# Two 4-block transpositions of a fused decoder kernel: from TensorE to block turns and moves

## The reference

```
y = rms(h) ; z = y @ w_in                      # 2048 -> 4096, in four mixers
oa = spatial unit(za)   : gelu(u) * (W_s @ layernorm(gelu(v)) + b_s)   # 512 wide
ob, oc, od              : short convolution, conformer, pooling        # 512 wide each
h = h + concat(oa, ob, oc, od) @ w_out         # the output projection
h = h + (silu(y @ w_gate) * (y @ w_up)) @ w_down
h = h + sigmoid(y @ w_ple_gate) * (p @ w_ple_proj) ; x1 = rms(h)
q, k, v, gate = rms(x1) @ swa_w_in             # the attention's input
h = x1 + (softmax(q k + bias, sinks) v * silu(gate)) @ swa_w_out
```

## Time and profile before

| | us |
|---|---|
| median of 3 runs | 1383.69 |
| lowest and highest | 1382.33, 1383.71 |
| the profiled execution, its own time | 1381.95 |
| its span | 1380.2 |
| TensorE busy in it | 1373.5 |
| VectorE busy | 1150.4 |
| ScalarE busy | 866.6 |

### The profile page before, as it was taken

The page is one execution under the profiler, slowest core; times in us unless marked ns, Lnnn a source line. Parts: engine busy times, 40 slices in busy tenths (PEclk is TensorE's granted clock), DMA queues, the critical chain, the costliest instruction groups (busy, mean ns, idle before and its releaser), DMA issues.

```text
span 1380.2 us, 16996 instructions
## 1 busy us (share of the span) xinstructions
PE 1373.5 (100%) x6191; PEld 1124.8 (81%) x6191; DVE 1150.4 (83%) x1394; ACT 866.6 (63%) x1162; POOL 152.2 (11%) x127
## 2 busy tenths in 40 slices
PE   9999999999999999999999999999999999999999
PEld 7888888888888888788888888888888887777887
DVE  6589976788999988899999889976777669886898
ACT  7476755566777555677756577655565556665554
POOL 2000010011111000111100011100000144430000
PEclk9999999999999999999999999999999999999999
DMA  9777656887999788899987889998878688889685
GB/s 332 249 209 216 199 174 228 284 234 252 297 277 267 226 260 256 249 279 264 280 267 248 245 255 251 276 321 295 253 236 279 219 263 259 262 257 289 204 251 173
DMA packets 181419, 349.80 MB, mean 253 GB/s; under 512 B 12913, under 2 KB 36717, under 8 KB 181208
## 3 DMA queue, kind: packets, MB, share of 16 engines
q1 hardware_dynamic: 158968, 289.56, 63.9%
q0 software_dynamic: 9280, 33.97, 12.6%
q10 hardware_dynamic: 13088, 25.18, 5.9%
HBM read 295.14 MB, written 26.26 MB: 233 GB/s over the span
## 4 chain that ended last, share of the span: by engine, by line
PE 96%; DVE 2%; DMA 1%; ACT 0%; issue 0%; POOL 0%; ACTq 0%; POOLq 0%; DVEq 0%
PE acc L2150 15%; PE acc L2152 14%; PE acc L2151 14%; PE acc L2334 13%; PE acc L2336 13%; PE acc L2337 13%; PE sp L2334 2%; PE sp L2336 2%; PE tp L2336 2%; PE tp L2334 2%; PE tp L2337 2%; PE sp L2337 2%; DMA wide<-w_raw 1%; DVE w_lo L1380 1%; PE acc L2212 1%; PE sp L2449 1%
## 5 line engine op out<-in xcount | busy, mean ns | idle before, releaser
L952 ACT ACTIVATE w_hi<-w_raw 128x1024 fp32r<-128x1024 f32 x453 | 474.2, 1057 | 310.2 <-PE acc L2152 209.7
L1380 DVE TENSOR_TENSOR w_lo<-w_raw,w_hi 128x1024 fp32r<-128x1024 f32 x431 | 522.3, 1226 | 155.0 <-ACT w_hi L952 152.4
L2150 PE MATMUL acc<-w_lo,hh 128*128 128x512 f32 x528 | 207.9, 394 | 0.0
L2152 PE MATMUL acc<-w_hi,hl 128*128 128x512 f32 x528 | 205.7, 390 | 0.0
L2151 PE MATMUL acc<-w_hi,hh 128*128 128x512 f32 x528 | 205.6, 389 | 0.0
L2334 PE MATMUL acc<-w_lo,yh 128*128 128x512 f32 x452 | 176.0, 389 | 0.0
L2336 PE MATMUL acc<-w_hi,yh 128*128 128x512 f32 x452 | 175.9, 389 | 0.0
L2337 PE MATMUL acc<-w_hi,yl 128*128 128x512 f32 x452 | 175.8, 389 | 0.0
L952 ACT ACTIVATE w_hi<-wide 128x1024 fp32r<-128x1024 f32 x104 | 110.3, 1060 | 72.0 <-DVE wide L1394 33.5
L1380 DVE TENSOR_TENSOR w_lo<-wide,w_hi 128x1024 fp32r<-128x1024 f32 x104 | 126.8, 1223 | 14.9 <-ACT w_hi L952 14.6
L2150 PE MATMUL acc<-w_lo,yh 128*128 128x512 f32 x352 | 137.4, 390 | 0.0
(11 more groups left out here) (336 smaller groups left out, 2180.3 us busy)
## 6 DMA issues: line engine op xcount, KB each, us to landing
w_raw<-in_w_gate SPq DMA_DIRECT2D x88, 512.0 KB, 5.7
w_raw<-in_w_up SPq DMA_DIRECT2D x88, 512.0 KB, 6.3
w_raw<-in_w_down SPq DMA_DIRECT2D x88, 512.0 KB, 6.4
w_raw<-in_w_in SPq DMA_DIRECT2D x64, 512.0 KB, 4.5
wide<-w_raw POOLq DMA_DIRECT2D x52, 512.0 KB, 5.7
w_raw<-in_swa_w_in ACTq DMA_DIRECT2D x48, 512.0 KB, 5.2
w_raw<-in_w_out SPq DMA_DIRECT2D x32, 512.0 KB, 5.5
w_raw<-in_w_ple_gate SPq DMA_DIRECT2D x32, 512.0 KB, 5.2
```

Source lines behind the costliest of these rows:

```text
L952: act.activation(w_hi[:, v % SPL], src, ACT.Copy).then_inc(hi_ready, 1)
L1380: dve.tensor_tensor(w_lo[:, v % SPL], src, w_hi[:, v % SPL].bitcast(F32), ALU.subtract).then_inc(lo_ready, 1)
L2150: pe.matmul(dst, xh[:, f, tk], w_lo[:, v % SPL, k], start=(f == 0), stop=False)
L2152: last = pe.matmul(dst, xl[:, f, tk], w_hi[:, v % SPL, k], start=False, stop=(f == CK * n - 1))
```

## The change

Both results are turned and moved instead of transposed on TensorE. The indices of the moved tiles go up by one (`T_OA = 0`, and a fourth `T_SWA`), the two pairs of PSUM halves go.

In the output projection `turn` follows the products on VectorE at (0, 0), the move stands on SP behind load 7, ScalarE's and VectorE's readings stay at (0, 3), and the first unit uses the spatial quarter last: short convolution, pooling, conformer, spatial.

In the attention `turn` follows `add_gated(3)` at (0, 3), the move stands on SP behind load 12, ScalarE makes the high half at (0, 6) and VectorE the low half at (0, 7), both behind the split of that step. The first two units are interleaved: chunks 0 to 5 of unit 0, 0 to 3 of unit 1, 6 and 7 of unit 0, 4 to 7 of unit 1. ScalarE takes unit 0 at (1, 7) instead of (1, 3).

```diff
+OUT_FIRST = (0, 1, 2, 3, 6, 7, 4, 5)
+SWA_STEPS = [(0, c) for c in range(6)] + [(1, c) for c in range(4)] + [(0, 6), (0, 7)] + [(1, c) for c in range(4, 8)]
+SWA_STEPS += [(v, c) for v in range(2, 9) for c in range(8)]
...
+LAST_CHUNK[SWA_UNIT] = OWN[START[SWA_UNIT] + SWA_STEPS.index((0, 7))] + 1
...
-T_FFN, T_HID, T_PLE, T_SWA, T_K, T_OG = 0, 4, 15, 19, 22, 23
+T_OA, T_FFN, T_HID, T_PLE, T_SWA, T_K, T_OG = 0, 1, 5, 16, 20, 24, 25
@@ SP
-                    load(START[OUT_UNIT + j] + c, wout_v, OUT_ROWS[c], CW * j)
+                    load(START[OUT_UNIT + j] + c, wout_v, OUT_ROWS[c if j else OUT_FIRST[c]], CW * j)
+                    if (j, c) == (0, 7):
+                        move(T_OA)
...
-                v, c = divmod(s, 8)
+                v, c = SWA_STEPS[s]
                 load(ATT + s, swi_v, CK * c, CW * SWA_ORDER[v])
                 if s == 4:
                     move(T_SWA + 2, freed=T_SWA)
+                if s == 12:
+                    move(T_SWA + 3, freed=T_SWA + 1)
@@ ScalarE
                     if (j, c) == (0, 3):
-                        high(H_OA, hh[:, 8:12])
+                        turned_high(T_OA, hh[:, 8:12])
...
-                    if (v, c) == (0, 5):
-                        high(H_SWA, hh[:, 12:16], gfs[:, 12:16])
+                    if (v, c) == (0, 6):
+                        swa_turned_high(3)
...
-                    if (v, c) == (1, 3):
+                    if (v, c) == (1, 7):
                         act.wait_ge(prod, 2)
                         take(SWA_UNIT, tok(0), ACT.Copy, rr)
@@ VectorE
                         last.then_inc(oa_ready, 1)
+                        dve.wait_ge(oa_ready, 1)
+                        turn(T_OA, tok(5))
...
-                        low(H_OA, hl[:, 8:12], hh[:, 8:12])
+                        turned_low(T_OA, hl[:, 8:12], hh[:, 8:12])
...
                     if (v, c) == (0, 3):
                         add_gated(3)
+                        dve.wait_ge(x1_ready, 4)
+                        turn(T_SWA + 3, resid[:, :, 3 * CW:])
                     if (v, c) == (0, 5):
-                        low(H_SWA, hl[:, 12:16], hh[:, 12:16], gfs[:, 12:16])
                         request(R_FIN, 32)
...
+                    if (v, c) == (0, 7):
+                        swa_turned_low(3)
@@ TensorE
-                for c in range(8):
-                    u = OUT_UNIT + j
+                for i in range(8):
+                    u, c = OUT_UNIT + j, i if j else OUT_FIRST[i]
...
                     if j == 0 and c == 4:
-                        wait_half_left(pe, H_OA + 1)
+                        pe.wait_ge(turned_lo, T_OA + 1)
...
-                    chunk(START[u] + c, u, c, hh, hl)
-                    if (j, c) == (0, 1):
-                        pe.wait_ge(oa_ready, 1)
-                        to_features(H_OA, tok(5))
+                    chunk(START[u] + i, u, c, hh, hl, end=None if j else OUT_FIRST[-1])
...
-                    if v == 0 and c in (0, 2, 4):
-                        pe.wait_ge(turned_lo, T_SWA + c // 2 + 1)
-                    if (v, c) == (0, 6):
-                        wait_half_left(pe, H_SWA + 1)
+                    if v < 2:
+                        j, k = SWA_STEPS[8 * v + c]
+                        if j == 0 and k % 2 == 0:
+                            pe.wait_ge(turned_lo, T_SWA + k // 2 + 1)
+                        chunk(START[u] + c, SWA_UNIT + j, k, hh, hl)
+                        continue
                     chunk(START[u] + c, u, c, hh, hl)
-                    if (v, c) == (0, 2):
-                        pe.wait_ge(x1_ready, 4)
-                        to_features(H_SWA, resid[:, :, 3 * CW:])
```

More of the change, by code:

```diff
@@ L222 @@
         LAST_CHUNK[_block.unit + _role] = _block.last(_role) + 1
-HALVES = "d" + "fx" + "xx" * 3 + "d" + "dx" + "aa" + "xx" + "dd" + "aa" + "xx"
-H_MIX, H_X, H_VEC, H_INIT, H_PZ, H_PO, H_CB, H_CN, H_OA = 0, 1, 9, 10, 12, 14, 16, 18, 20
+HALVES = "d" + "fx" + "xx" * 3 + "d" + "dx" + "aa" + "xx" + "dd" + "aa"
+H_MIX, H_X, H_VEC, H_INIT, H_PZ, H_PO, H_CB, H_CN = 0, 1, 9, 10, 12, 14, 16, 18
 M_HC, M_SC, M_BG = range(3)
-H_SWA = len(HALVES)
-HALVES += "xx"
 H_Q, H_PV = {}, {}
@@ L2138, in _, with chunk @@
         def _(pe):
-            def chunk(s, u, c, xh, xl, by_bank=None):
+            def chunk(s, u, c, xh, xl, by_bank=None, end=None):
                 if c == 0 and u >= 2:
@@ L2144, in chunk @@
                 wait_low(pe, v)
-                n = UNITS[u][0]
+                end = UNITS[u][0] - 1 if end is None else end
                 for t in range(T):
@@ L2152, in chunk @@
                         last = pe.matmul(dst, xl[:, f, tk], w_hi[:, v % SPL, k], start=False,
-                                         stop=(f == CK * n - 1))
+                                         stop=(f == CK * end + CK - 1))
                     if by_bank is not None:
```

## The result

The change makes the kernel slower: a median of 1386.43 us over 8 runs (1385.77 to 1389.00) against 1383.53 over 8 runs of the kernel before (1382.33 to 1385.11). The ratio is 1.0028, with a 95% interval of 1.0019 to 1.0037: 3.9 us, between 2.6 and 5.1. The medians lie 2.9 apart, against the +3.1 that was forecast. The profiled execution took 1386.48 around a span of 1384.4; the kernel before, 1381.95 around 1380.2.

The account below looks back on a forecast made before the run. TensorE, busy in all of the span, was taken to bound the kernel. No gain from the first removal, +0.5 and +2.6 us from the moves (0.92 returned included) gave +3.1: 1386.8 us, range 1384.3 to 1389.7.

Parts of the forecast that it names:

- The removal at the first place: Output projection: dropping the transposes gains 0, as step 2 waits for the same low half; bounds 0 and 0.9 us.
- The first move: Output projection: the spatial tile returns at 213.4, delaying step 4's weights queued behind it; +0.5 us, bounds 0 and +3.4.
- The second move: Attention: the late tile holds up weights of steps 7 and 8; +2.6 us net, bounds +2.0 and +3.2, +5.5 with slow reads.
- Not slower: Rival, attention step 8: the tile returns before ScalarE asks, a move of 6.0 us instead of 9.1; 1383.3, chance 0.2.
- The clock falls: Rival: the 2.8 us wait puts TensorE at 1.2 GHz for a chunk, 2.7 us more; 1389.5, chance 0.1.
- The sum: Both places: +0.5 and +2.6 make +3.1 us, 1386.8 in terms of the median; forecast's own span +2.0 to +4.4.
- What was priced at nothing: Interleaved units, unit 0 taken four chunks later, the attention tile's low half before step 10: each covered, 0.
- the 0.92: Attention: TensorE time of the eight removed transposes, 0.92 us, said to come back and already counted in the +2.6.

Follow-up runs that it names:

- second_alone: The changed kernel with only the attention's edits, the spatial unit's output transposed on TensorE again: median 1387.26 us, 1.0031 of the kernel before.
- move_behind_11: The changed kernel with SP's move of the attention's last quarter behind load 11 instead of load 12: median 1382.16 us, 0.9999 of the kernel before.
- late_tables: `late_and_early_split` with the second and third of GpSimd's bias tables sent later: median 1381.53 us, 0.9993 of the kernel before.
- late_halves: The changed kernel with ScalarE's and VectorE's halves of the attention's fourth tile made later, at (1, 1): median 1383.02 us, 1.0005 of the kernel before.
- late_and_early_split: `late_halves` with ScalarE's conformer work in the output projection one step later, behind step 2's high half: median 1382.90 us, 1.0000 of the kernel before.
- first_alone: The changed kernel with only the output projection's edits, the attention's last quarter transposed on TensorE again: median 1382.78 us, 0.9998 of the kernel before.

## Why the prediction was right, and where not

**The removal at the first place, 0:** right. Step 2 waits for the same low half, 0.74 in the change and 0.77 alone, and starts at 210.93 instead of 210.89.

**The first move, +0.5:** wrong, it cost 0. The step that failed is "The nearest write, at 1052.17, landed in 4.4". This one landed in 2.64, with nothing else being moved (the DMA engines' share is 0.00 ahead of its first byte, see the end); the tile came at 211.83 instead of 213.4, ScalarE waited 0.18 for it, and TensorE has no wait at step 4. The lower bound had named the condition ("0 if the write lands half a microsecond sooner").

**The second move, +2.6:** right in place and size. The put went out at 1073.21 (1073.3), the write took 4.88 (5.0), the tile was there at 1082.53 (1082.4), the wait was 2.92 (2.8), and the cost without the clock, in `second_alone`, 2.59. The wait for the tile on ScalarE and the weights queued behind it are the way it went. That 5.0 was taken over 4.4, with a load right ahead, carried this.

**Not slower:** the rival did not come, but its mechanism is the right one. It asked for a move of 6.0 instead of 9.1; one load sooner the move took 1081.64 - 1074.80 = 6.84 and began 1.5 sooner, and the loss was gone. The rival's sum is 0.4 off: 1086.6 is where the attention would win the 0.5 of the first place, and the whole 0.92 needs step 8 at 1083.5 + 2.72 = 1086.2, a move of 5.6.

**The clock falls:** given 0.1, and it came in the profiled run and, by the mean granted clock, in most of the others, on top of the wait and not in its stead. Its price was half of the 2.7 that was given: step 7 took 1090.94 - 1086.49 = 4.45 instead of some 2.8, 1.6 more, of which some 0.4 would have been waited for step 8's low half anyway (step 7 of `second_alone` took 1090.69 - 1087.46 = 3.23). Setting it as a rival to the forecast was the mistake; a wait on the engine that bounds the kernel has to be priced together with what it does to the clock.

**The sum:** 0 + 2.6 + 1.3 is 3.9, which the profiled execution shows between steps 0 and 8, against +3.1. It came out near partly by luck: the first move was priced 0.5 too high and the clock, 1.3, not at all. 0.3 more lies outside the span (below). The upper end of the forecast's own span, +4.4, doesn't follow from the bounds beside it; +0.5 and +3.2 are 3.7.

**What was priced at nothing** stayed so in the change: the interleaved units, unit 0 taken later, the tile's low half before step 10. That the 0.92 "comes back" holds only if nothing stands right behind it: in `move_behind_11` and `late_tables` it came back, in `late_halves` and `late_and_early_split` the keys' transfer, 0.3 us from being late before, took it.

## What to carry to other kernels

The time of a turn and a move varied here with that of its write, and the write with what was in flight ahead of it: 2.64 us on idle queues, 4.9 behind one load, 6.7 behind three. So place the put ahead of a load rather than behind it, and ask for the tile at the latest step that still serves. On an engine that is always busy, price a wait with the clock behind it, and look for the next wait before a saving is counted.

## What was not expected of the hardware

- **A write on idle queues.** Windows of the change at the first write, issued at 204.99 and landed by 207.63:

```profile
205.40:205.80 0.40, 0.40 (x3) 0.33 (x2) 0.40 (x1) 0.39 (x2) 0.00 (x0) 1.00 0.00 0
205.80:206.20 0.40, 0.40 (x3) 0.35 (x2) 0.27 (x1) 0.40 (x1) 0.00 (x0) 1.00 0.99 399
206.60:207.00 0.40, 0.40 (x4) 0.31 (x3) 0.00 (x0) 0.40 (x2) 0.00 (x0) 1.00 1.03 420
207.00:207.20 0.20, 0.20 (x3) 0.16 (x2) 0.00 (x0) 0.20 (x2) 0.00 (x0) 1.00 0.47 185
```

  The 512 KB move from 205.8 to 207.1, with 0.8 us before the first byte and 0.5 behind the last. The Trainium skill, "DMA: Bandwidth & Descriptors", section Anatomy of one DMA — SWDGE (gpsimd) path, gives a fixed cost of 2.0 us, most of it behind the last byte, for transfers from GpSimd; by its formula an estimate for 512 KB is 3.2. This write, from SP's queue, has a fixed part of 1.3, and most of that ahead of the first byte.
- **0.3 us outside the span.** An execution's own time was 2.03 to 2.11 above its span in all 8 runs of the change, 2.1 in that of `second_alone` and `late_tables`, but 1.75 in the kernel before and 1.8 in `first_alone`. It goes with the attention's edits; what it is, the profile doesn't show.
- **The clock behind short waits.** About the same wait left it at 1.00 once (2.84 us) and at 0.55 another time (2.92 us).
